# Modulation weights of the last layer summed on VectorE with TensorE adding over partitions, and the other layer's modulation units taken in fours

## The reference

```python
DEPTH, D_MODEL = 2, 1024
# w_mod: (DEPTH, 1024, 6 * 1024); c and c_ctx: one vector of 1024 each
for l in range(DEPTH):
    last = l == DEPTH - 1
    mod = (jax.nn.silu(c) @ w_mod[l] + b_mod[l])[:, None, :]
    mod_c = jax.nn.silu(c_ctx) @ w_mod[l] + b_mod[l]
    sh1, sc1, ga1, sh2, sc2, ga2 = jnp.split(mod, 6, axis=-1)
    csh1, csc1, cga1, csh2, csc2, cga2 = jnp.split(mod_c, 6, axis=-1)
    h = modulate(rms_norm(x, g_pre_mix[l]), sh1, sc1)
    hc = modulate(rms_norm(xc, g_pre_mix[l]), csh1, csc1)
    ...
    x = x + ga1 * rms_norm(o, g_post_mix[l])
    f = conv_ffn(modulate(rms_norm(x, g_pre_ffn[l]), sh2, sc2), w_up[l], conv_w[l], conv_b[l], w_down[l])
    x = x + ga2 * rms_norm(f, g_post_ffn[l])
    if not last:
        ...   # the context tokens are carried on, with cga1, csh2, csc2, cga2
```

## Time and profile before

| | us |
|---|---|
| median of 3 runs | 2728.67 |
| lowest and highest | 2728.22, 2731.36 |
| the profiled execution, its own time | 2730.54 |
| the span of its trace | 2728.8 |
| PE busy, share of the span | 2613.9, 96% |
| DVE busy | 1668.7, 61% |
| ACT busy | 1384.1, 51% |
| mean granted clock of PE, of full speed | 0.987 |

### The profile page before, as it was taken

One profiled execution on the slowest core, in us unless ns is written; L12 is line 12 of the kernel. 1 busy time (PEld: TensorE's weight loads), 2 busy tenths in 40 slices (PEclk: granted clock), 3 DMA queues, 4 the chain that ended last, 5 costly groups with the idle time before them and its releaser, 6 DMA issues.

```text
span 2728.8 us, 40372 instructions
## 1 busy us (share of the span) xinstructions
PE 2613.9 (96%) x14676; PEld 2125.0 (78%) x14676; DVE 1668.7 (61%) x2518; ACT 1384.1 (51%) x2241; POOL 104.1 (4%) x112
## 2 busy tenths in 40 slices
PE   8999999998999999899999999999999899999998
PEld 7768888676888888778876777778777678667997
DVE  5665545756998999445555544653454457456776
ACT  5645435654777777433435453532333544455655
POOL 2000001000000000000000100100000110010000
PEclk9999999999999999999999999999999899999999
DMA  7439795445999998332331224453553244334464
GB/s 229 132 125 277 250 313 162 126 131 171 320 332 324 326 317 303 95 78 62 85 89 55 75 65 128 124 178 124 163 166 96 78 109 132 96 105 138 141 193 155
DMA packets 353481, 448.03 MB, mean 164 GB/s; under 512 B 19872, under 2 KB 198176, under 8 KB 353312
## 3 DMA queue, kind: packets, MB, share of 16 engines
q1 hardware_dynamic: 349792, 435.44, 50.9%
q0 software_dynamic: 3232, 9.97, 1.3%
q10 hardware_dynamic: 288, 0.36, 0.0%
HBM read 444.63 MB, written 1.08 MB: 163 GB/s over the span
## 4 chain that ended last, share of the span: by engine, by line
PE 85%; DVE 7%; ACT 4%; issue 3%; DMA 1%; DVEq 0%; POOL 0%; SPq 0%; ACTq 0%; POOLq 0%
PE ps L2512 21%; PE ps L2499 18%; PE ps L2560 17%; PE ps L2573 8%; PE ps L2564 4%; PE ps L2878 2%; PE ps L2889 2%; PE ps L2581 2%; PE ps L2768 2%; PE ps L2909 2%; PE ps L2453 2%; DVE w_lo L1632 1%; PE ps L2599 1%; ACT w_hi L1103 1%; PE ps L2871 1%
## 5 line engine op out<-in xcount | busy, mean ns | idle before, releaser
L1632 DVE TENSOR_TENSOR w_lo<-raw,w_hi 128x1024 fp32r<-128x1024 f32 (+1 forms) x578 | 686.2, 1198 | 531.4 <-ACT w_hi L1103 449.5
L1103 ACT ACTIVATE w_hi<-raw 128x1024 fp32r<-128x1024 f32 (+1 forms) x578 | 589.9, 1031 | 319.9 <-PE ps L2512 128.8
L2560 PE MATMUL ps<-w_hi,h_hi 128*128 128x512 f32 (+1 forms) x992 | 403.8, 409 | 12.8 <-DVE h_lo L2123 6.5
L2560 PE MATMUL ps<-w_hi,h_lo 128*128 128x512 f32 (+1 forms) x992 | 379.9, 385 | 0.0
L2499 PE MATMUL ps<-h_hi,w_hi 128*128 128x256 f32 (+1 forms) x1008 | 300.4, 323 | 0.0
L2573 PE MATMUL ps<-w_lo,h_hi 128*128 128x512 f32 (+1 forms) x992 | 298.2, 384 | 0.0
L2499 PE MATMUL ps<-h_lo,w_hi 128*128 128x256 f32 (+1 forms) x1008 | 296.0, 319 | 0.0
L2560 PEld LDWEIGHTS ps<-w_hi,h_hi 128*128 128x128 f32 x992 | 187.4, 189 | 71.2 <-issue 31.8
L2499 PEld LDWEIGHTS ps<-h_hi,w_hi 128*128 128x128 f32 x1008 | 191.6, 190 | 30.3 <-issue 16.1
L2573 PEld LDWEIGHTS ps<-w_lo,h_hi 128*128 128x128 f32 x992 | 183.3, 188 | 39.5
L2560 PEld LDWEIGHTS ps<-w_hi,h_lo 128*128 128x128 f32 x992 | 187.5, 189 | 29.5 <-issue 1.0
(11 more groups left out here) (317 smaller groups left out, 4153.9 us busy)
## 6 DMA issues: line engine op xcount, KB each, us to landing
raw<-in_w_in SPq DMA_DIRECT2D x196, 512.0 KB, 3.7
arena<-in_w_mod SPq DMA_DIRECT2D x96, 512.0 KB, 5.6
raw<-in_w_up SPq DMA_DIRECT2D x88, 512.0 KB, 4.3
raw<-in_w_gu_exp SPq DMA_DIRECT2D x64, 512.0 KB, 5.5
arena<-in_w_gu_exp SPq DMA_DIRECT2D x64, 512.0 KB, 4.9
arena<-in_w_gu_exp SPq DMA_DIRECT2D x64, 384.0 KB, 3.9
arena<-in_w_dn_exp SPq DMA_DIRECT2D x48, 512.0 KB, 6.3
raw<-in_w_gu_dense SPq DMA_DIRECT2D x44, 512.0 KB, 7.4
```

Of the source, the lines that this page charges most:

```text
L1103: nc.scalar.activation(w_hi[:, half, 0:n], place[:, 0:n], ACT.Copy).then_inc(seg.sig.hi_ready, 1)
L1632: nc.vector.tensor_tensor(w_lo[:, half, 0:n], place[:, 0:n], w_hi[:, half, 0:n].bitcast(F32), ALU.subtract).then_inc(seg.sig.lo_ready, 1)
L2560: ins = mm(ps[:, 2 * h + p % 2, 0:width], x[:, k + c, p * P:(p + 1) * P], wh[:, c * width:(c + 1) * width], start=opens and c == 0 and x i ...
```

## The change

In the convolutional feed-forward there are no modulation units any more. `SummedMods` lays out instead 48 parts of `w_mod_2[1]`, each 128 rows by 1024 columns (512 KB), in the order of pieces `MOD_ORDER` (2, 3, 4, 5, 0, 1) and eight parts for a piece. SP loads a part into one of three places when DVE has used the part three before it (`load_parts`). DVE multiplies each part by the entry of `cond` that belongs to the partition and adds it to a running sum of 128 by 1024 (`add_parts`, called right behind `split` for unit j): for pieces 2 to 5 for the token vector alone, for pieces 0 and 1 for both vectors, which makes 4 x 8 + 2 x 16 = 64 operations in units 2 to 52 of the segment's 68. There are three places for sums. When a piece is complete, `spread_sums` on PE adds over the partitions: four matmuls of 32 by 256 for each of the 8 sums, behind units 8, 16, 23, 37, 39 and 52. ACT copies the rows at fixed units instead of behind the last modulation unit, and `mod_cols` takes them in their new places.

In the dense feed-forward the 24 modulation units of a pass stand in fours after the first half of every second block. What they load and compute is as before.

```diff
+MOD_ORDER, MOD_BOTH, MOD_GAP, ONE_AT, MOD_PACE = (2, 3, 4, 5, 0, 1), 2, 2, 16, (0.95, 0.65, 0.7)
...
+class SummedMods:
+    def __init__(self, weights, iters, n, ups, places, sums, one):
+        self.weights, self.places, self.sums, self.one = weights, places, sums, one
+        self.steps, self.loads, self.shut, self.last, self.ends = {}, {}, {}, {}, []
+        spent = 2.0
+        for u in range(len(MOD_ORDER) * DC):
+            if u == (len(MOD_ORDER) - 1) * DC:
+                spent += MOD_GAP
+            at = int(spent)
+            self.steps.setdefault((at // n, at % n), []).append(u)
+            self.loads.setdefault(at + 1, []).append(u)
+            spent += self.sides(u // DC) * MOD_PACE[0 if at < ups + 2 else 1 if at < n else 2]
...
-                these = mods[len(mods) * b // FB:len(mods) * (b + 1) // FB]
+                these = [] if b % 2 else mods[2 * b:2 * b + 4]
...
+            def load_parts(seg, it, j):
+                sm = seg.summed
+                for u in sm.loads.get(it * seg.n + j, ()):
+                    if u < 3:
+                        sp.wait_ge(split_done, seg.clear)
+                    else:
+                        sp.wait_ge(part_added, sm.added(u - 3))
+                    r, k = u // DC, u % DC
+                    sp.dma_start(sm.places[u % 3], sm.weights[k * P:(k + 1) * P, MOD_ORDER[r] * D:(MOD_ORDER[r] + 1) * D]).then_inc(parts_loaded[u % 3], 16)
...
+            def add_parts(seg, it, j):
...
+                for u in sm.steps.get((it, j), ()):
+                    r, k = u // DC, u % DC
+                    dve.wait_ge(parts_loaded[u % 3], 16 * (u // 3 + 1))
+                    w = sm.places[u % 3]
+                    for s in range(sm.sides(r)):
+                        n = sm.sum_no(r, s)
+                        dst, by = sm.sums[n % 3], cond[:, k, COND + s:COND + s + 1]
+                        if k == 0:
+                            if n >= 3:
+                                dve.wait_ge(sum_spread, n - 2)
+                            ins = nc.vector.tensor_scalar(dst, w, by, None, ALU.mult)
+                        else:
+                            dve.wait_ge(part_added, sm.added(u - 1) - sm.sides(r) + s + 1)
+                            ins = nc.vector.scalar_tensor_tensor(dst, w, by, dst, ALU.mult, ALU.add)
+                        ins.then_inc(part_added, 1)
...
+            def spread_sums(seg, it, j):
+                sm = seg.summed
+                for r in sm.shut.get((it, j), ()):
...
+                    for s in range(sm.sides(r)):
+                        n = sm.sum_no(r, s)
+                        pe.wait_ge(part_added, sm.added(r * DC + DC - 1))
+                        row = 2 * (r - sm.first[it]) + s
+                        for g in range(4):
+                            ins = mm(ps[32 * g:32 * g + 32, 2, 0:2 * P], sm.one[:, ONE_AT - row:ONE_AT - row + 32],
+                                     sm.sums[n % 3][:, g * 2 * P:(g + 1) * 2 * P], start=r == sm.first[it] and s == 0,
+                                     stop=ends and s == sm.sides(r) - 1)
+                        ins.then_inc(sum_spread, 1)
```

More of the change, by code:

```diff
@@ L208, in loaded, with sides, added, sum_no @@
         return 16 * ((self.unit0 - self.apart + it * self.splits + self.split_at[j]) // RAW)
+class SummedMods:
[10 more added lines that the diff above has]
+            spent += self.sides(u // DC) * MOD_PACE[0 if at < ups + 2 else 1 if at < n else 2]
+            if u % DC == DC - 1:
+                self.ends.append(at)
+        for r, at in enumerate(self.ends):
+            at = at if at < ups + 4 else max(at, n + 3)
+            self.shut.setdefault((at // n, at % n), []).append(r)
+        phases = [[r for g, rs in self.shut.items() for r in rs if g[0] == it] for it in range(iters)]
+        self.first = [min(p) for p in phases] + [len(MOD_ORDER)]
+        for it, p in enumerate(phases):
+            at = next(g for g, rs in self.shut.items() if max(p) in rs)
+            self.last[it, at[1] + AHEAD] = self.sum_no(max(p) + 1, 0)
+    def sides(self, r):
+        return 2 if MOD_ORDER[r] < MOD_BOTH else 1
+    def added(self, u):
+        return sum(self.sides(i // DC) for i in range(u + 1))
+    def sum_no(self, r, s):
+        return sum(self.sides(i) for i in range(r)) + s
 class Step:
@@ L362, in build @@
         mods_done = sem("mods_done")
+        parts_loaded = [sem(f"parts_loaded_{i}") for i in range(3)]
+        part_added = sem("part_added")
+        sum_spread = sem("sum_spread")
         split_hi_done = sem("split_hi_done")
@@ L890, in second_layer @@
             seg.tail = Step("tail", dict(count), rows=mod_rows if more else None, l=l + 1)
+            if more:
+                seg.summed = SummedMods(a["w_mod_2"][l + 1], seg.iters, seg.n, 2 * FB, [view(i * UNIT, UNIT) for i in range(3)],
+                                        [view(at, UNIT) for at in (3 * UNIT, NQK_AT, FREE + 6656)], view(FREE + 7680, ONE_AT + 32))
             seg.gains = gains(1, l, nq // TT, view(FREE + 4096, 2, D))
@@ L1410, in body @@
                             continue
+                        if seg.summed is not None and (it, j) in seg.summed.last:
+                            act.wait_ge(sum_spread, seg.summed.last[it, j])
+                            nc.scalar.activation(seg.mod_rows[it], ps[:, 2, 0:2 * P], ACT.Copy).then_inc(mod_saved, 1)
                         for i in seg.behind(j):
@@ L2163, in body @@
                             continue
+                        if seg.summed is not None:
+                            add_parts(seg, it, j)
                         for i in seg.behind(j):
@@ L2813, in body @@
                         use(seg, it, j, first)
+                        if seg.summed is not None:
+                            spread_sums(seg, it, j)
                         if seg.mode == "moe":
```

35 lines of the change are left out of this document (29 added, 6 removed).

## The result

| | before | changed |
|---|---|---|
| median, first comparison (4 runs each) | 2730.02 us | 2704.91 us (2701.24 to 2708.30) |
| ratio, 95% interval | | 0.9903 (0.9891 to 0.9916) |
| median, second comparison (7 and 4 runs) | 2730.86 us | 2704.46 us (2703.93 to 2705.65) |
| ratio, 95% interval | | 0.9905 (0.9889 to 0.9922) |
| the profiled execution, and its span | 2730.54, 2728.8 us | 2701.24, 2699.4 us |

The change makes the kernel 1% faster: 25.1 us by the first medians, 26.4 by the second. Forecast were 26.5 us and 2702.2 us.

What follows compares the result with a forecast made beforehand. PE was taken to bound both changed segments, with loads close behind in the dense one. Terms -29.4 + 5.9 - 3.0 = -26.5 us, from the median 2728.67, gave 2702.2 us; range 2698 to 2708, with rival A 2697 to 2713.

Steps and rivals of the forecast that it cites:

- terms 1 and 2: Convolutional feed-forward: 22 modulation groups leave PE, -29.4 us; 8 sums in 6 groups are added on PE, +5.9 us.
- term 5: Dense feed-forward: 12 of 21 modulation groups are left with the same 48 units, 9 x 0.33 = 3.0 us saved.
- Term 3: Convolutional segment: 64 new DVE operations, 78 us together, cost nothing because DVE's idle time hides them.
- The room: Convolutional segment, second pass: DVE may free a block's banks 6.8 us later before PE waits; 3.6 us delay expected.
- rival B: Convolutional segment: DVE becomes the bound, deciding from 1.6 us per new operation; 2740 us at 2.46 us; chance 0.04.
- Term 4: Convolutional segment: new waits of SP for DVE before part loads, and of ACT for sums, cost nothing.
- The cover: Dense segment, second pass: the tightest raw load's 3.7 us of room holds against 3.3 us of two more modulation loads.
- Rival A: Dense segment: loads in fours make raw loads late, term 5 becomes 0 to +8 us, 2705 to 2713 us; chance 0.13.
- Rival C: Both segments: gain is only the removed weight loads' busy time, 8.1 us, nothing in the dense one; 2720.6 us; chance 0.05.

Runs made afterwards that it cites:

- half more: Changed kernel, with two extra unread 456-column DVE operations behind every second part's operations; convolutional segment 383.75 us, 5.58 more than in the changed kernel.
- the work doubled: Changed kernel, with two extra unread DVE operations behind every one of the 56 running additions; convolutional segment 412.91 us, 34.7 more; whole 2741.16 us.
- groups of six: Changed kernel, with the dense segment's modulation units in sixes instead of fours, still five places; dense segment 251.78 us, 48.98 more.

## Why the prediction was right, step by step

**The total.** 2702.2 us was forecast, 2704.9 and 2704.5 measured, faster by 25.1 and 26.4 us for 26.5. The sum is right to 0.1 us in the segments, with some luck: 0.2 us too little for terms 1 and 2 and 0.2 too much for term 5 cancel. What the medians differ by beyond that is within what the rest of the program varies by from one profiled execution to the next. The profiled execution of the first comparison, 29.4 us shorter in span, was lucky by 2.9 us in the rest (2118.4 against 2121.3), so its own time says less about the forecast than the medians do.

**Terms 1 and 2** stood at -29.4 and +5.9, -23.5 together; measured -23.73. The price of a group was measured by itself, 0.44 us (forecast 0.42); that of a unit or a sum is what is then left, 0.417 (forecast 0.42). Working the price out from the pace between units, and not from the group's busy time, is what made it right.

**Term 3**, 78 us of DVE at no cost: PE has no wait for DVE or `w_hi` in the segment, so the step holds. Its sizes were off both ways. The running sum takes 1.280 us, not 1.23. The first product takes 0.748 us, not 1.1. Together 56 x 1.280 + 8 x 0.748 = 77.7 us; the errors cancelled. The room was underrated. With the prices measured in the two runs with more work (1.28 and 1.38 us, 0.75 for a first product) the formula of rival B gives 1.8 and 11.0 us for the two passes with half more, and 14.2 and 24.9 with the work doubled; measured were 0.8 and 4.8, and 13.1 and 21.6, the last with some 6 us in it that the slower clock cost. So the first pass comes out within about 1 us, and the second is overrated by 6 us with half more and by 3 with the work doubled, or some 10 without the clock's share. That the doubled run came near its forecast is partly luck: the extra work was dearer than supposed, the room larger, and the clock was left out. Why the second pass has more room than 6.8 us stays open.

**Term 4**, waits that come with it, at nothing: SP's wait for `part_added` delays nothing that PE needs. The waits over 1730 to 2090 us, three rows of all engines and one of SP:

```profile
ACT act_hi L1341 <- DVE arena L1975: 48.8, 22, 3.7
ACT arena L1339 <- DVE arena L1781: 36.0, 21, 3.2
...
ACT w_hi L1161 <- DMA raw<-in_w_down: 3.4, 1, 3.4
...
SPq L1004 <- DVE arena L1716: 117.4, 33, 6.4
```

SP stood up to 6.4 us before a part's load, where the prediction allowed one operation of 1.23; some of that it would have stood for a raw place anyway, and ACT waited for a raw load once in the whole stretch. ACT now waits 48.8 us for DVE's activation, 23.5 before. None of it reaches PE in the change; with DVE's extra work doubled, waits for ACT's `w_hi` did.

**Term 5**, -3.0 in the dense segment: -2.79, 0.31 us for a group and not 0.33. One figure of its working was wrong: PE does not need about 71 us for the units of a pass that bring modulation but, by the prediction's own prices, 11 x 5.75 + 24 x 0.43 + 6 x 0.33 = 75.6, and the trace has 75.7 (328.38 to 404.05 us). So PE and the 77 us of loads were all but even, and the loss of 8 us, had loads set the pace, was overrated. The cover held with more room than I had left: the tightest unit after, against the earlier trace rows, in ACT's and PE's timelines:

```profile
344.31 1.06 ACT L1161 ACTIVATE w_hi<-raw 128x1024 fp32r<-128x1024 f32 x1 [8.34 <-DMA raw<-in_w_gu_dense]
...
346.78 0.39 PE L2615 MATMUL ps<-h_hi,w_hi 128*128 128x256 f32 x1
```

Ready at 345.37 and used at 346.78: 1.41 us of room, where 3.70 were and I had left 0.4. In the second profiled execution the same unit had 2.46 us (ready at 347.04, used at 349.50), so this room varies by a microsecond. The idle time in the bracket nearly doubled, 8.34 us for 4.31: the raw load stands in the queue behind four modulation loads. The median of a load to its landing went from 7.4 to 8.4 us:

```profile
arena<-in_w_mod SPq DMA_DIRECT2D x40, 512.0 KB, 6.6
raw<-in_w_gu_dense SPq DMA_DIRECT2D x39, 512.0 KB, 8.4
```

**Rival A** (loads late, chance 0.13) did not come in the change; the room shrank by 2.3 us and stayed above nothing. With groups of six it came: 34 us of waits, and 49 us with the slower clock behind them. I had priced it at +8 at most for the change, from average rates, and that bound would have been wrong by far had the queue been blocked: average rates do not price a queue that stands still.

**Rival B** (DVE the bound, 0.04) is refuted for the change and confirmed as a mechanism. At 1.28 us for a sum the change is on the safe side of the 1.6 us at which I let it decide. With 1.38 us more work for 32 of the 56 running sums, 2.1 us on average, it cost 5.6 us, and with 1.38 us more for each it made the kernel slower than before.

**Rival C** (a gain by the share of weight loads, 0.05) is refuted: 8 us forecast, 26.5 measured in the segments. PEld stands at 78% of the span before and after, and PE had nothing to spare. The Trainium skill, "Perfetto Trace Analysis", section "Identifying the Most-Contended Engine", asks for MFU and the busy share of the weight loads in place of matmul busy time. Here the share of 79% had to be held against the 83% that this stream can show at most; taken as a plain headroom of a fifth it would have misled.

## What to carry to other kernels

Price what sits between two stretches of a bound engine by the pace around it, with and without it, and split it into a price for each piece and a price for each interruption; here 0.42 and 0.44 us, and they held for an operation that no trace had shown. Before work is moved to an engine with idle time, look for the one operation in its order that frees something for the bound engine, and count how late that may come; and before loads are bunched, count the places, since the load that needs a place of its own group stops the whole queue. A wait of the bound engine costs more than its length where the clock falls with it; with groups of six the clock added half of the idle time again. Where an edit is worth less than the program's own variation, compare the lengths of the segments it touches and not the spans.

## What the runs showed of the hardware

- `TENSOR_SCALAR` on 128 by 1024 float32 from scratch memory took 0.748 us, the running sum of the same shape 1.280. The 128 by 512 `TENSOR_SCALAR` of the kernel before took 0.592 us, so doubling its columns looked like 1.1 us and was not. The Trainium skill, "VectorE: DVE Perf Modes", section "Mode 2×_2P — use both read ports for one tensor", says that an operation with one tensor source in SBUF can give two results a cycle and one with two tensor sources cannot. The 0.748 against 1.280 us agrees with it; why the 512 columns took 0.592 is left open.
- A unit of four-quadrant matmuls with 32-column weights costs 0.417 us of PE, and going to them and back 0.44 us among 512-column matmuls (22 groups against 12) and 0.31 to 0.32 us among 256-column ones (12, 21 and 39 groups). Why the two differ was not tried.
- With groups of six, PE waited 4.8 us on average at seven places, and the granted clock went to 1.2 GHz each time: 47.8 us of the 251.8 at that level, an estimated 17 us of delay. In the changed kernel, where PE waits for nothing in this segment, it stayed at 2.4 GHz for all of the 202.8 us.
- Segments bounded by PE repeat to 0.02 us from run to run, while the rest of the same program varies by 6.6 us.
